# FFN gate and up: main and low activations as one 512-column product, halves joined by ACT and DVE

## The reference

```python
def swiglu(h, w_gate_up, w_down):
    gate, up = jnp.split(h @ w_gate_up, 2, axis=-1)
    return (jax.nn.silu(gate) * up) @ w_down

# first kind, per layer
h = rms_norm(x, norm_ffn_g[i])
x = x + swiglu(h, ffn_w_gate_up[i], ffn_w_down[i])
# second kind, twice per layer
h = h + 0.5 * swiglu_ffn(rmsnorm(h, norm_ffn[i]), w_ffn_in[i], w_ffn_out[i])
```

## Time and profile before

| | us |
|---|---|
| median of 3 runs | 2574.54 (2573.38 to 2581.89) |
| span of the profiled execution | 2575.1 |
| PE busy | 2467.8 |
| weight loads (PEld) busy | 2410.2 |
| DVE busy | 1778.5 |
| ACT busy | 1260.1 |

### The profile page before, as it was taken

How to read it: one execution, slowest core, us unless ns; L and a number is a source line. 1 busy time by engine, 2 the same in 40 slices (tenths; PEclk the granted TensorE clock), 3 DMA queues, 4 the chain that set the end, 5 groups by cost and what they waited for, 6 DMA issues and landing times.

```text
span 2575.1 us, 54629 instructions
## 1 busy us (share of the span) xinstructions
PE 2467.8 (96%) x23198; PEld 2410.2 (94%) x23198; DVE 1778.5 (69%) x2300; ACT 1260.1 (49%) x1508; POOL 220.8 (9%) x246
## 2 busy tenths in 40 slices
PE   7999779999999899999999999999999999999998
PEld 7999669999999889989999999999999998999998
DVE  5998956665555666657666669976667667986665
ACT  5444535335666553344344346565334335675433
POOL 5000140003000100000000000600000000330000
PEclk9999879999999899999999999999999999999999
DMA  5553024555676735535545544434555554434453
GB/s 216 181 200 122 19 84 177 190 191 190 172 179 175 171 121 193 194 139 180 195 179 196 195 173 150 150 135 165 196 195 180 196 195 147 157 141 150 186 191 127
DMA packets 65839, 430.76 MB, mean 167 GB/s; under 512 B 8288, under 2 KB 11360, under 8 KB 15904
## 3 DMA queue, kind: packets, MB, share of 16 engines
q1 hardware_dynamic: 58864, 410.30, 44.0%
q0 software_dynamic: 6000, 17.46, 4.5%
q10 hardware_dynamic: 832, 0.92, 0.1%
HBM read 426.45 MB, written 1.15 MB: 166 GB/s over the span
## 4 chain that ended last, share of the span: by engine, by line
PE 85%; DVE 8%; ACT 4%; issue 2%; DMA 0%; DVEq 0%; ACTq 0%
PE psum L2018 26%; PE psum L2019 25%; PE psum L2020 25%; DVE w_lo L1332 2%; ACT w_hi L847 1%; PE psum L2063 1%; PE psum L2228 1%; PE psum L2134 1%; PE psum L2377 1%; PE psum L2365 1%; DVE h L1351 1%; DVE h_lo L1340 1%; PE psum L2355 1%; PE psum L2321 0%; PE psum L2117 0%
## 5 line engine op out<-in xcount | busy, mean ns | idle before, releaser
L2018 PE MATMUL psum<-h_hi,w_hi 128*128 128x256 f32 x4320 | 1212.7, 281 | 16.8 <-DVE h_lo L1376 9.6
L2019 PE MATMUL psum<-h_lo,w_hi 128*128 128x256 f32 x4320 | 1202.4, 278 | 0.0
L2020 PE MATMUL psum<-h_hi,w_lo 128*128 128x256 f32 x4320 | 1202.0, 278 | 0.0
L1332 DVE TENSOR_TENSOR w_lo<-raw,w_hi 128x2048 fp32r<-128x2048 f32 x387 | 888.3, 2296 | 377.7 <-ACT w_hi L847 377.5
L847 ACT ACTIVATE w_hi<-raw 128x2048 fp32r<-128x2048 f32 x387 | 741.5, 1917 | 819.9 <-PE psum L2020 819.8
L2018 PEld LDWEIGHTS psum<-h_hi,w_hi 128*128 128x128 f32 x4320 | 817.0, 189 | 26.1 <-issue 19.1
L2019 PEld LDWEIGHTS psum<-h_lo,w_hi 128*128 128x128 f32 x4320 | 816.9, 189 | 0.5 <-issue 0.5
L2020 PEld LDWEIGHTS psum<-h_hi,w_lo 128*128 128x128 f32 x4320 | 816.4, 189 | 0.0
L2018 PE MATMUL psum<-act_hi,w_hi 128*128 128x256 f32 x1536 | 425.4, 277 | 0.7 <-DVE act_lo L1895 0.7
L2020 PE MATMUL psum<-act_hi,w_lo 128*128 128x256 f32 x1536 | 424.4, 276 | 0.0
L2019 PE MATMUL psum<-act_lo,w_hi 128*128 128x256 f32 x1536 | 424.4, 276 | 0.0
(11 more groups left out here) (334 smaller groups left out, 2359.6 us busy)
## 6 DMA issues: line engine op xcount, KB each, us to landing
raw<-in_panels SPq DMA_DIRECT2D x387, 1024.0 KB, 4.8
arena<-bias_by_distance POOLq DMA_DIRECT2D x32, 384.0 KB, 6.2
x<-in_x SPq DMA_DIRECT2D x1, 1024.0 KB, 5.7
arena<-in_s_cbd POOLq DMA_DIRECT2D x4, 256.0 KB, 2.9
arena<-in_s_b SPq DMA_DIRECT2D x1, 1024.0 KB, 15.2
arena<-in_s_c SPq DMA_DIRECT2D x1, 1024.0 KB, 17.1
hidden<-in_s_cbd POOLq DMA_DIRECT2D x4, 256.0 KB, 2.9
arena<-arena POOLq DMA_DIRECT2D x32, 32.0 KB, 1.9
```

The costliest lines, as they stand in the source:

```text
L1332: v.tensor_tensor(w_lo[:, s, :], raw[:, s, :], w_hi[:, s, :].bitcast(F32), ALU.subtract).then_inc(lo_ready, 1)
L2018: t.matmul(o, w[0], xin[0], start=start, stop=False, skip_group_check=True)
L2019: t.matmul(o, w[0], xin[1], start=False, stop=False, skip_group_check=True)
L2020: return t.matmul(o, w[1], xin[0], start=False, stop=stop, skip_group_check=True)
```

## The change

`h_hi` and `h_lo` become two halves of one tile `h_hl`, per channel block main beside low, 512 columns in a row. In gate and up, a new function `wide` takes the place of `project`. For each weight block it runs one matmul of 512 columns, main weights by main and low activations, into a whole PSUM bank, and one of 256 columns, low weights by main activations, added to the second half of that bank. The main product is then in the first half and both corrections in the second. A gate panel fills banks 0 and 1 and an up panel banks 2 and 3, in every chunk. After each panel ACT copies the two correction halves to SBUF (`corr`, new, 128x512), and DVE adds the main halves to them and then scales, two operations instead of one. PE waits, per panel, for the add of the chunk before (`halves_added`) instead of for the product of two chunks before (`act_ready`). Since all of banks 0 to 3 are in use, the sum of squares moves to bank 4, and the clearing of banks 4 to 7 moves from ahead of the sum to behind the up panel and the wait for the root. Down panels and all other stages keep their three matmuls; they read `h_hi` and `h_lo` as views of the new tile.

```diff
@@ -137,8 +137,8 @@
         eps = sb("eps", [P, 1])
         eps_head = sb("eps_head", [P, 1])
         warm = sb("warm", [P, 1])
-        h_hi = sb("h_hi", [P, KT, S], F32R)
-        h_lo = sb("h_lo", [P, KT, S], F32R)
+        h_hl = sb("h_hl", [P, KT, 2, S], F32R)
+        h_hi, h_lo = h_hl[:, :, 0], h_hl[:, :, 1]
         rstd = sb("rstd", [P, S])
 
         hidden = sb("hidden", [P, 2, 2, 2, S])
...
@@ -891,6 +895,11 @@
             def ffn(st):
                 n0, f = st["n0"], st["ffn"]
 
+                def corr(c, p, n, i=None):
+
+                    a.wait_ge(panel_done, p + n + 1 if i is None else i * 6 + p + n + 1)
+                    a.activation((act if n else gate)[:, c % 2], psum[:, 2 * n:2 * n + 2, S:2 * S], ACT.Copy).then_inc(corr_copied, 1)
+
                 def silu(c, p, i=None):
 
                     def at(v, per):
@@ -904,14 +913,18 @@
                         a.wait_ge(act_ready, f * FFC + c + 1 if i is None else i * 2 + f * FFC + c + 1)
                         a.activation(act_hi[:, c % 2], act[:, c % 2], ACT.Copy).then_inc(act_hi_ready, 1)
 
+                corr(0, n0, 0)
                 split(n0 + 3)
+                corr(0, n0, 1)
                 silu(0, n0)
                 high(0)
                 with a.Fori(0, (FFC - 1) // 2) as i:
                     for c in (1, 2):
                         p = hidden_panel(n0, c)
                         split(p + 2, i, 6)
+                        corr(c, p, 0, i)
                         split(p + 3, i, 6)
+                        corr(c, p, 1, i)
                         silu(c, p, i)
                         split(p + 4, i, 6)
                         high(c, i)
...
@@ -1383,13 +1396,20 @@
 
                 rstd_2 = rstd[:, :].unsqueeze(1).to_broadcast([P, 2, S])
 
-                def tiles(b):
-                    return bank[b % PROJ_BANKS][:, :].rearrange("p (t s) -> p t s", t=2)
+                def main(n):
+
+                    return psum[:, 2 * n:2 * n + 2, 0:S]
 
                 def scale_gate(c, p, i=None):
 
-                    v.wait_ge(panel_done, p + 1 if i is None else i * 6 + p + 1)
-                    v.tensor_tensor(gate[:, c % 2], tiles(2 * c), rstd_2, ALU.mult).then_inc(scaled, 1)
+                    def at(val, per):
+                        return val if i is None else i * per + val
+                    b = c % 2
+                    v.wait_ge(panel_done, at(p + 1, 6))
+                    v.wait_ge(corr_copied, at(2 * (f * FFC + c) + 1, 4))
+                    v.tensor_tensor(gate[:, b], main(0), gate[:, b], ALU.add).then_inc(halves_added, 1)
+                    v.wait_ge(halves_added, at(2 * (f * FFC + c) + 1, 4))
+                    v.tensor_tensor(gate[:, b], gate[:, b], rstd_2, ALU.mult).then_inc(scaled, 1)
 
                 def hidden(c, p, i=None):
 
@@ -1397,7 +1417,10 @@
                         return val if i is None else i * per + val
                     b = c % 2
                     v.wait_ge(panel_done, at(p + 2, 6))
-                    v.tensor_tensor(act[:, b], tiles(2 * c + 1), rstd_2, ALU.mult).then_inc(scaled, 1)
+                    v.wait_ge(corr_copied, at(2 * (f * FFC + c) + 2, 4))
+                    v.tensor_tensor(act[:, b], main(1), act[:, b], ALU.add).then_inc(halves_added, 1)
+                    v.wait_ge(halves_added, at(2 * (f * FFC + c) + 2, 4))
+                    v.tensor_tensor(act[:, b], act[:, b], rstd_2, ALU.mult).then_inc(scaled, 1)
                     v.wait_ge(scaled, at(2 * (f * FFC + c) + 2, 4))
                     v.wait_ge(gate_ready, at(f * FFC + c + 1, 2))
                     v.tensor_tensor(act[:, b], gate[:, b], act[:, b], ALU.mult).then_inc(act_ready, 1)
@@ -2060,12 +2083,29 @@
                 for b in range(4):
                     t.wait_ge(sq_ready, 4 * n + b + 1)
                     for c in (2 * b, 2 * b + 1):
-                        last = t.matmul(bank[SUMS_BANK[False]][:, 0:S], ones[:, :], h[:, c, :],
+                        last = t.matmul(bank[4][:, 0:S], ones[:, :], h[:, c, :],
                                         start=(c == 0), stop=(c == KT - 1))
                 last.then_inc(ss_ready, 1)
 
             def ffn(st):
                 n0, f = st["n0"], st["ffn"]
+
+                def wide(p, n, i=None, per=0, parts=None, led=None):
+
+                    t.wait_ge(lo_ready, p + 1 if i is None else i * per + p + 1)
+                    for k, m in [(k, m) for k in range(KT) for m in range(2)] if parts else \
+                            [(k, m) for m in range(2) for k in range(KT)]:
+                        if parts and m == 0 and k % 2 == 0:
+                            t.wait_ge(parts[0], parts[1] + k // 2 + 1)
+                        o = bank[2 * n + m]
+                        if led and (m, k) in led:
+                            lead(o, k == 0, led[m, k])
+                        w = weights(p, k * COLS + m * P)
+                        t.matmul(o[:, :].rearrange("p (x s) -> p x s", x=2), w[0], h_hl[:, k], start=(k == 0), stop=False,
+                                 skip_group_check=True)
+                        last = t.matmul(o[:, S:2 * S], w[1], h_hi[:, k], start=False, stop=(k == KT - 1),
+                                        skip_group_check=True)
+                    last.then_inc(panel_done, 1)
 
                 def down(c, p, i=None):
 
@@ -2082,23 +2122,24 @@
                                 last.then_inc(sums_ready, 1)
                     last.then_inc(panel_done, 1)
 
-                project(n0, 0, parts=(h_lo_ready, 4 * st["hs"]))
+                wide(n0, 0, parts=(h_lo_ready, 4 * st["hs"]))
                 t.wait_ge(const_set, 4)
+                t.wait_ge(sq_added, 3 * (st["hn"] - st["whole"]))
+                t.matmul(bank[4][:, 0:S], ones[:, :], h[:, 0], start=True, stop=True).then_inc(ss_ready, 1)
+                wide(n0 + 1, 1, led=PACE)
+                t.wait_ge(rms_ready, st["hn"] + 1)
                 for b in range(4):
 
                     t.matmul(bank[4 + b][:, :].rearrange("p (a m) -> p a m", m=P), zeros[:, :],
                              zeros[:, :].unsqueeze(1).to_broadcast([P, 4, P]), start=True, stop=True)
-                t.wait_ge(sq_added, 3 * (st["hn"] - st["whole"]))
-                t.matmul(bank[SUMS_BANK[True]][:, 0:S], ones[:, :], h[:, 0], start=True, stop=True).then_inc(ss_ready, 1)
-                project(n0 + 1, 1, led=PACE)
-                t.wait_ge(rms_ready, st["hn"] + 1)
                 with t.Fori(0, (FFC - 1) // 2) as i:
                     for c in (1, 2):
                         p = hidden_panel(n0, c)
 
-                        t.wait_ge(act_ready, i * 2 + (f * FFC + c - 1))
-                        project(p, 2 * c, i, 6)
-                        project(p + 1, 2 * c + 1, i, 6)
+                        t.wait_ge(halves_added, i * 4 + 2 * (f * FFC + c - 1) + 1)
+                        wide(p, 0, i, 6)
+                        t.wait_ge(halves_added, i * 4 + 2 * (f * FFC + c - 1) + 2)
+                        wide(p + 1, 1, i, 6)
                         down(c - 1, p + 2, i)
                 down(FFC - 1, n0 + 32)
 
```

More of the change, by code:

```diff
@@ L172, in build @@
         gate_ready = sem("gate_ready")
+        corr_copied = sem("corr_copied")
+        halves_added = sem("halves_added")
         scaled = sem("scaled")
@@ L306, in build, with sums_bank @@
         y_of = [bank[4 + o // 2][:, (o % 2) * S:(o % 2 + 1) * S] for o in range(KT)]
-        SUMS_BANK = {True: 3, False: 4}
+        def sums_bank(st):
+            return 3 if st["cols"] else 4
         def hidden_panel(n0, c):
@@ L880, in norm @@
                 root, sums = (da.rstd, slice(0, 2)) if st["cols"] else (rstd[:, :], slice(0, S))
-                a.activation(root, bank[SUMS_BANK[st["late"]]][:, sums], ACT.Sqrt, bias=eps[:, 0:1],
+                a.activation(root, bank[sums_bank(st)][:, sums], ACT.Sqrt, bias=eps[:, 0:1],
                              scale=1.0 / D).then_inc(rms_ready, 1)
@@ L1359, in norm @@
                     for w, e in enumerate((E * EPS, EPS)):
-                        v.tensor_scalar(da.eps[:, w], bank[SUMS_BANK[True]][:, 0:2], e / D, e * EPS, ALU.mult, ALU.add)
+                        v.tensor_scalar(da.eps[:, w], bank[sums_bank(st)][:, 0:2], e / D, e * EPS, ALU.mult, ALU.add)
                     v.reciprocal(da.rstd, da.rstd).then_inc(rstd_ready, 1)
@@ L2399, in dilated_mixer @@
                         for qt in range(2):
-                            last = t.matmul(bank[SUMS_BANK[True]][:, qt:qt + 1], h[:, 0, qt::2], ones[:, 0:1],
+                            last = t.matmul(bank[sums_bank({"cols": True})][:, qt:qt + 1], h[:, 0, qt::2], ones[:, 0:1],
                                             start=True, stop=True)
```

## The result

The changed kernel takes 2651.87 us (median of 4 runs, 2641.05 to 2653.13) against 2576.18 of the kernel before beside it (4 runs): ratio **1.028, 95% interval 1.0267 to 1.0294**. The forecast was 2594, the range 2577 to 2620: the direction holds, the size doesn't.

A forecast was written before the change was run, and what follows sets the result against it. TensorE was taken to bound the kernel, with DVE becoming the first FFN's bound. Terms of 13.5 + 0 + 0 + 5.9 = 19.4 us on the profiled 2575.1 gave 2594.5, forecast as 2594 us, range 2577 to 2620.

The forecast's parts named there:

- Part 1: Gate and up matmuls, three become two: 340 ns per triple as before, cost 0, bounds -3 and +13 ns.
- Rival 2: Clearing between PACE and the loop leaves the slow pace, 353 ns per triple: 2642 us, half of it 2618; chance 0.10.
- Rival 3: Weight loads bound PE in the loop, so the pair costs 325 ns, 15 less: -35 us, 2559; chance 0.12.
- rival 4: 6.7 ns belong to each matmul instruction, so one less per triple saves 16 us: 2578; chance 0.12.
- Rival 1: Low bound of the pair in gate and up, 338 ns, 2.7 less per triple: 2588 us; chance 0.16.
- Part 2: First FFN, two more DVE operations per chunk: DVE becomes the bound, 13.5 us longer, bounds 10 and 15.
- Part 3: Other seven FFNs, the added DVE operations and ACT copies: covered by PE, cost 0; about 7 us if a cover failed.
- Part 4: Clearing of four banks moved behind the up panel: 6 x 0.92 + 0.37 = 5.9 us, 0.37 in the second FFN.
- The sign: Whole kernel: slower, with chance 0.76, against 0.12 for faster and 0.12 for the same.

The follow-up runs named there:

- three of 256: Changed kernel with three 256-column matmuls instead of each pair in gate and up: 2651.35 us; with the clearing also back in its old place, 2596.90 us.
- groups of eight: Changed kernel with the clearing in its old place, gate and up running eight 512-column, then eight 256-column matmuls per output block: 2606.88 us.
- the run with the filled wait: Kernel before, first FFN's two DVE scalings per chunk done twice, plus 28 matmuls on zeros ahead of its last down panel: 2588.58 us.
- clearing late: Kernel before with only the clearing of banks 4 to 7 moved behind the up panel and the wait for the root: 2639.62 us.
- the run without the third small matmul: Kernel before without the up panel's third small matmul (2 columns on zeros, in PACE): 2631.79 us.
- the run with the double scaling: Kernel before, in whose first FFN DVE does each of the two scalings of a chunk twice, the second waiting for the first: 2596.07 us.

## Why the prediction was wrong, point by point

- **Part 1, matmul pace: the step that failed.** I took 340 ns for the pair and named 353 as the bound; it is 353 in the loops and 349 right behind the clearing. At 13 ns more, 2,352 products are 31 us, and the down panels, which the sum left out, add 16. The error was not the columns' price but the assumption that the loop would keep the quick pace. The trace of before held the warning: 117.8 ns ahead of the clearing, and 224 to 236 ns from one of its wide matmuls to the next. I read L2089 as a price list and not as a stream that might leave TensorE at the other pace.
- **Rival 2** had the mechanism, the clearing between `PACE` and the loop, and the price: 47 us against 7 x 31 x 0.21 = 46 in the trace. I gave it 0.10, because in the FFNs of the kernel before the pace never gets lost; there no wide matmul stands behind the small one. It lacked that the pair would lose the pace anyway (2642.54 with the clearing in its old place), so either cause alone gives nearly the whole loss, and they don't add up.
- **Rival 3, weight loads, and rival 4, a cost per matmul:** wrong. PEld fell from 94% to 88% busy and nothing was won; three of 256 and pairs under the same late clearing take the same time (2651.35 and 2651.87).
- **Rival 1** (338 ns) no run shows. The Trainium skill's "TensorE: Matmul & The Clock Gate" (Back-to-back issue gap) gives N / 2.4 + 2.5 ns for the gap of an isolated matmul, by which 512 columns take an estimated 215.8 ns. The traces have 224 at the least between two wide matmuls and 229 on the mean in groups of eight, so that level isn't met with this type at any place here.
- **Part 2, first FFN: the sum was right, what follows it was missing.** Its chunk is 17.23 us (17.22 expected), the last down panel starts at 248.62 instead of 234.46, 14.2 later (13.5). Beyond that the panel lasts 7.3 us instead of 5.4 (0.2 of it by the slow pace), since TensorE stood still for 3.6 us ahead of it and the granted clock fell, to 0.76 on the mean of the panel. The S5 stage up to the end of its first panel takes 138.1 instead of 135.0, with a clock of 0.50 at 274 us, behind a wait of 1.5 us that stands in both traces and left it at 1.00 before. So 14 grew to 18. The Trainium skill's "TensorE: Matmul & The Clock Gate" (HAM oscillation) says that waits between bursts of matmuls bring TensorE to its lower clock; the run with the filled wait agrees, with 1.00 where 0.65 stood without the filling.
- **Part 3, the other FFNs' copies and adds at 0:** right (three of 256, clearing first).
- **Part 4, the clearing at 5.9 us:** near for the kernel before, too low for the changed one. The seven FFNs are 54.8 us longer with the clearing behind and 45.5 with it ahead, both with pairs, 9.3 apart: 1.0 each in FFNs 4 to 7 and 0.8 in the last (0.92 foreseen), but 2.1 in the third and 2.4 in the second, where I had 0.37. In the kernel before, both times at the slow pace (clearing late against the run without the third small matmul), the seven are 7.9 apart, 1.6 of it that small matmul: 6.3, with 0.5 in the second. Its indirect price, the lost pace, is what matters: 2651.35 against 2596.90 with three of 256, 54 us, of which 46 are the pace and some 8 its own.
- **The sign** held, by terms whose sum, 19 us, was a quarter of the loss.

**Still open.** What inside TensorE keeps a pace isn't settled. The small matmul worked wherever 36 matmuls of 256 columns went ahead of it, with 12 ahead in all down panels that had it but only in four FFNs of eight where the clearing stood ahead of those 12, never directly behind pairs or the clearing, and yet in all eight directly behind four wide matmuls of a group. The small matmul and the wide ones aren't the only switches either: in the first FFN of the run with the double scaling, which has only 256-column matmuls there, the down panel of chunk 0 is at the quick pace and those of chunks 1 to 9 are at the slow one. Between them TensorE waits 2.2 us for DVE, goes on at the quick pace, has 3.4 us at a clock of 0.50, and comes out of that at the slow pace. Whether the pair could hold 340 ns if it were ever reached isn't known, as no run reached it for a whole panel. Nor is why the second and third FFN paid 2 us for the clearing in the changed kernel.

## What to carry to other kernels

Where a trace shows one matmul form at two steady paces, treat the pace as a state: find what switches it and ask of each edit what it puts between the switch and the loop, even an edit that saves instructions. A dense stream of equal matmuls kept it here, a mix of widths didn't, and a long group of wide ones changed it. And price a new wait of TensorE not only by its length but by the clock behind it. Filling one such wait with idle matmuls, ahead of it and not behind, took 7.5 us off here; at the two mixes no gain is shown.

## What the runs showed of the hardware that I had not expected

- The same 256-column float32r matmul runs at 113.3 or 117.8 ns at a granted clock of 1.00 for hundreds of us, and a pair of 2-column matmuls in front moves it from the slow to the quick one (55 us for the kernel).
- Four 512-column matmuls on zeros move it back (and leave the slow pace as it is), while behind the groups of eight the pace is 118.0 and 113.4 ns by turns. Pairs of 512 and 256 columns take 349 or 353 ns, groups of eight 344.6 per product, three of 256 340 or 353: fewer matmuls, no less time than at the quick pace.
- 3.6 us of stillness cost some 5 us more in the changed kernel (1.6 in the panel behind it beyond its slow pace, 3.1 in S5), and 7.5 in the one with the double scaling, where filling it won them back. Behind it, and behind a short wait some 20 us on, the granted clock was 0.50 for 3.4 to 6.8 us.
